# Retention layer of a hybrid decoder: four sample states updated during the attention, queries weighed on VectorE

## The reference, cut to what matters

```python
q = _rotate(...); k = _rotate(...) * (RET_DK ** -0.5)
o = intra + inter                     # prompt: chunks; sample: one token
# for a sample (T = 1) this is, per head, with g = 1 - 2**(-5-h):
#   S_new = g * S_old + k^T v         (256 x 512), stored
#   o     = q @ S_new                 (512)
o = o * rsqrt(mean(o * o) + EPS)
o = o.reshape(B, T, vd) * silu(gate)
return o @ w_out, S
```

## Time and profile before

| | |
|---|---|
| Time, median of 3 runs | 2841.74 us (2841.07 to 2852.38) |
| The profiled execution's own time | 2859.43 us |
| Its span | 2857.9 us |
| TensorE busy (matmul) | 2704.7 us, 95% |
| VectorE busy | 1282.3 us, 45% |
| ScalarE busy | 796.0 us, 28% |
| GpSimd busy | 288.5 us, 10% |
| Mean granted TensorE clock | 0.963 |
| Chain that ended last | PE 87%, DVE 7%, issue 3%, ACT 2% |

### The profile page before, as it was taken

How to read it: one execution, slowest core, us unless ns; L and a number is a source line. 1 busy time by engine, 2 the same in 40 slices (tenths; PEclk the granted TensorE clock), 3 DMA queues, 4 the chain that set the end, 5 groups by cost and what they waited for, 6 DMA issues and landing times.

```text
span 2857.9 us, 49322 instructions
## 1 busy us (share of the span) xinstructions
PE 2704.7 (95%) x20961; PEld 2591.1 (91%) x20961; DVE 1282.3 (45%) x1577; ACT 796.0 (28%) x935; POOL 288.5 (10%) x305
## 2 busy tenths in 40 slices
PE   7999999999999999999999999898879888999997
PEld 6999997989898899999999999788878787999997
DVE  5444234535353554433444423665546654544333
ACT  3222222323232432222322222332223222322222
POOL 1000010101010110000100000004410342100000
PEclk9999999999999999999999999998989899999998
DMA  4332333525152433322333223220012100233231
GB/s 120 88 88 84 87 101 109 174 66 182 60 182 66 141 89 88 88 80 86 111 96 95 79 79 107 70 69 21 25 65 75 47 30 19 77 99 89 70 91 61
DMA packets 340962, 246.82 MB, mean 86 GB/s; under 512 B 9540, under 2 KB 322044, under 8 KB 340832
## 3 DMA queue, kind: packets, MB, share of 16 engines
q1 hardware_dynamic: 326480, 197.32, 23.6%
q0 software_dynamic: 14352, 47.58, 5.0%
HBM read 218.81 MB, written 26.05 MB: 86 GB/s over the span
## 4 chain that ended last, share of the span: by engine, by line
PE 87%; DVE 7%; issue 3%; ACT 2%; DMA 0%; SPq 0%; POOLq 0%; POOL 0%; ACTq 0%; DVEq 0%
PE ps L684 57%; PE ps L864 13%; PE ps L1024 6%; PE ps L785 2%; PE ps L756 1%; PE ps L762 1%; DVE cv L1699 1%; ACT wh L1164 1%; PE ps L721 1%; DVE wl L1417 1%; PE ps L975 1%; PE ps L982 0%; PE ps L987 0%; DMA raw<-in_ffn_gu_dram 0%; PE ps L1070 0%
## 5 line engine op out<-in xcount | busy, mean ns | idle before, releaser
L1417 DVE TENSOR_TENSOR wl<-raw,wh 128x2048 fp32r<-128x2048 f32 (+1 forms) x204 | 427.5, 2095 | 389.6 <-ACT wh L1164 389.6
L684 PE MATMUL ps<-xh,wh 128*128 128x260 f32 x2816 | 569.5, 283 | 4.7 <-DVE gate L1882 4.4
L684 PE MATMUL ps<-xh,wl 128*128 128x260 f32 x2816 | 568.6, 284 | 0.0
L684 PE MATMUL ps<-xl,wh 128*128 128x260 f32 x2816 | 567.9, 283 | 0.0
L1164 ACT ACTIVATE wh<-raw 128x2048 fp32r<-128x2048 f32 (+1 forms) x204 | 354.4, 1737 | 355.9 <-PE ps L684 224.9
L684 PEld LDWEIGHTS ps<-xh,wh 128*128 128x128 f32 x2816 | 435.9, 189 | 6.3 <-issue 5.2
L684 PEld LDWEIGHTS ps<-xh,wl 128*128 128x128 f32 x2816 | 435.5, 189 | 0.0
L684 PEld LDWEIGHTS ps<-xl,wh 128*128 128x128 f32 x2816 | 434.3, 189 | 0.0
L684 PE MATMUL ps<-hh,wh 128*128 128x260 f32 x1408 | 287.9, 286 | 13.4 <-DVE hl L1887 13.4
L684 PE MATMUL ps<-hh,wl 128*128 128x260 f32 x1408 | 286.0, 285 | 0.0
L684 PE MATMUL ps<-hl,wh 128*128 128x260 f32 x1408 | 285.9, 285 | 0.0
(11 more groups left out here) (326 smaller groups left out, 3016.5 us busy)
## 6 DMA issues: line engine op xcount, KB each, us to landing
raw<-in_ffn_gu_dram SPq DMA_DIRECT2D x176, 512.0 KB, 5.0
raw<-in_ffn_down_dram SPq DMA_DIRECT2D x64, 384.0 KB, 3.5
raw<-in_ret_w_in_dram SPq DMA_DIRECT2D x48, 512.0 KB, 4.5
raw<-in_ffn_down_dram SPq DMA_DIRECT2D x64, 320.0 KB, 4.0
s_ring<-in_state_ret_dram POOLq DMA_DIRECT2D x32, 512.0 KB, 4.7
out_dram<-s_ring POOLq DMA_DIRECT2D x32, 512.0 KB, 5.1
raw<-in_gdn_w_in_dram SPq DMA_DIRECT2D x32, 512.0 KB, 4.6
raw<-in_ret_w_out_dram SPq DMA_DIRECT2D x16, 512.0 KB, 4.4
```

Source lines behind the costliest of these rows:

```text
L684: m_ = nc.tensor.matmul(ps[:, 2 * q + h, 0:HALF], w_, v[:, kt0 + t, h * HALF:(h + 1) * HALF], start=b_, stop=e_)
L1417: nc.vector.tensor_tensor(wl[:, s, 0:cols], raw[:, s, 0:cols], wh[:, s, 0:cols].bitcast(F32), ALU.subtract).then_inc(w_low, 1)
```

## The change

- Values 0 to 3 are spread after the prompt's outputs 1 and 2, into banks 0 to 3. Values 4 and 5 take the old place of 0 and 1, values 6 and 7 stand in gate unit 9.
- States 0 to 3 are decayed before the v copies of ScalarE, updated by VectorE during the prompt's outputs and sums, and stored by GpSimd's queue between its sums of squares. All four places of the ring are reloaded after the last sum.
- VectorE weighs each updated state with the query: c is half 0 times q's first 128 values, d is half 1 times the other 128 plus c. The sum lies in `sq`, `ssq`, a spare place under `yh`, or `osum`. TensorE then sums over partitions with a column of ones: four tiles of weights, not eight.
- Queries 0 to 3 stand in gate unit 8, queries 4 to 7 in unit 10, each in twos; the samples' norm comes one step of 128 earlier in unit 11.
- u and w are now the two instructions of an update, each counted.

```diff
-RET_T = Steps("p0 p1 p23 k01 v0 v1 v2 k23 v3 vs o0 o1 o2 o3 s0 s1 n "
-              "b0 b1 b2 b3 q0 q1 b4 b5 q2 q3 b6 b7 q4 q5 q6 q7 ns")
-RET_V = Steps("q k pt0 pt1 pt23 k01 k23 vlo ro u0 u1 on0 u2 u3 y0 lo0 on1 u4 u5 y1 lo1 on2 u6 u7 y2 lo2 on3 "
+RET_T = Steps("p0 p1 p23 k01 v0 v1 v2 k23 v3 vs o0 o1 b0 b1 o2 b2 b3 o3 s0 s1 n "
+              "b4 b5 q0 q1 q2 q3 b6 b7 q4 q5 q6 q7 ns")
+RET_V = Steps("q k pt0 pt1 pt23 k01 k23 vlo u0 w0 u1 w1 c0 c1 d0 d1 u2 w2 u3 w3 c2 c3 d2 d3 ro "
+              "on0 u4 w4 u5 w5 c4 c5 d4 d5 y0 lo0 on1 u6 w6 u7 w7 c6 c7 d6 d7 y1 lo1 on2 y2 lo2 on3 "
...
-RET_A = Steps("v0 v1 v2 v3 vs o0 sq0 o1 sq1 o2 sq2 o3 sq3 s0 s1 root "
-              "g0 g1 g2 g3 silu0 hi0 g4 g5 silu1 hi1 g6 g7 silu2 hi2 rs silu3 hi3")
+RET_A = Steps("g0 g1 g2 g3 v0 v1 v2 v3 vs o0 sq0 o1 sq1 o2 sq2 o3 sq3 s0 s1 root "
+              "g4 g5 silu0 hi0 g6 g7 silu1 hi1 silu2 hi2 rs silu3 hi3")
...
+        def weighed(b):
+
+            return (sq[:, 0, 0:RV], sq[:, 1, 0:RV], ssq[:, 0:RV], spare[:] if b < RING else osum[:])[b % RING]
+
+        def value_bank(b):
+
+            return b if b < RING else 4 + b % 2
...
 # GpSimd
+                    if e >= 2:
+                        for b in (2 * e - 4, 2 * e - 3):
+                            store(b)
...
+                for c in range(RING):
+                    pool.wait_ge(s_stored[c], 32 * h + 16)
+                    pool.wait_ge(ret_v, RET_V(f"d{c}", h))
+                    pool.sem_inc(pool_held, 1)
+                    pool.dma_start(s_ring[:, c], state(ret_in, c + RING)).then_inc(s_landed[c], 16)
...
+                for b in range(RING, DEC):
+                    store(b)
...
 # TensorE
+                    if e in (1, 2):
+                        value(2 * e - 2)
+                        value(2 * e - 1)
...
-                    pe.wait_ge(ret_v, RET_V(f"u{b}", h))
+                    pe.wait_ge(ret_v, RET_V(f"d{b}", h))
                     for e in range(4):
-                        for t in range(2):
-                            m_ = nc.tensor.matmul(ps[:, 7, e * DEC + b:e * DEC + b + 1],
-                                                  s_ring[:, b % RING, t, e * P:(e + 1) * P],
-                                                  rq[:, t, SEQ + b:SEQ + b + 1], start=t == 0, stop=t == 1)
+                        m_ = nc.tensor.matmul(ps[:, 7, e * DEC + b:e * DEC + b + 1], weighed(b)[:, e * P:(e + 1) * P],
+                                              ones[:, 0:1], start=True, stop=True)
...
                     if g == 0:
                         in_products(*unit, range(0, 2))
+                        query(0)
+                        query(1)
                         in_products(*unit, range(2, 5))
+                        query(2)
+                        query(3)
...
+                    elif g == 1:
+                        in_products(*unit, range(0, 5))
+                        value(6)
+                        value(7)
...
+                    elif g == 2:
+                        in_products(*unit, range(0, 2))
+                        query(4)
+                        query(5)
+                        in_products(*unit, range(2, 5))
+                        query(6)
+                        query(7)
...
+                        in_products(*unit, range(0, 6))
                         pe.wait_ge(ret_v, RET_V("ossq", h))
...
 # ScalarE
+                act.wait_ge(head_landed, 16 * h + 16)
+                for b in range(RING):
+                    decay(b)
                 for c in range(4):
                     act.wait_ge(ret_t, RET_T(f"v{c}", h))
...
+                    for b in ((4, 5), (6, 7), (), ())[g]:
+                        decay(b)
...
+                    if g == 0:
+                        act.wait_ge(ret_t, RET_T("q3", h))
...
 # VectorE
+                def weigh(b, half):
+
+                    if half == 0:
+                        if b >= RING:
+                            dve.wait_ge(ret_t, T(f"q{b - RING}", h))
+                        dve.wait_ge(ret_v, V(f"u{b}", h))
+                        nc.vector.tensor_scalar(weighed(b), s_ring[:, b % RING, 0, :], rq[:, 0, SEQ + b:SEQ + b + 1], None, ALU.mult)\
+                            .then_inc(ret_v, V.did(f"c{b}"))
+                    else:
+                        dve.wait_ge(ret_v, V(f"c{b}", h))
+                        nc.vector.scalar_tensor_tensor(weighed(b), s_ring[:, b % RING, 1, :], rq[:, 1, SEQ + b:SEQ + b + 1], weighed(b),
+                                                       ALU.mult, ALU.add).then_inc(ret_v, V.did(f"d{b}"))
...
+                update_two(0)
+                update_two(2)
                 split_next(4)
...
-                    if g < 3:
-                        update(2 * g + 2)
-                        update(2 * g + 3)
+                    if g < 2:
+                        update_two(2 * g + 4)
```

More of the change, by code:

```diff
@@ L343, in build @@
             rinv_s = sb("rinv_s", [P, DEC], stack=st)
+            with ExitStack() as before_yh:
+                spare = sb("spare", [P, RV], stack=before_yh)
             yh = sb("yh", [P, 4, NTOK], F32R, stack=st)
@@ L534, in ret_body, with store @@
                     pool.dma_start(s_ring[:, b], state(ret_in, b)).then_inc(s_landed[b], 16)
+                def store(b):
+                    pool.wait_ge(ret_v, RET_V(f"w{b}", h))
+                    pool.sem_inc(pool_held, 1)
+                    pool.dma_start(state(ret_new, b), s_ring[:, b % RING]).then_inc(s_stored[b % RING], 16)
                 for e in range(4):
                     pool.wait_ge(ret_a, RET_A(f"sq{e}", h))
+                    if e >= 2:
+                        for b in (2 * e - 4, 2 * e - 3):
+                            store(b)
                     if e == 0:
@@ L751, in ret_body, with value @@
                 pe.wait_ge(ret_a, RET_A("vs", h))
+                def value(b):
+                    if b == 0:
+                        pe.wait_ge(ret_v, RET_V("vlo", h))
+                    elif b in (4, 5):
+                        pe.wait_ge(ret_a, RET_A(f"s{b - 4}", h))
+                    elif b in (6, 7):
+                        pe.wait_ge(ret_v, RET_V(f"w{b - 2}", h))
+                    both = pick[:, b:b + 1].broadcast_to([LOW + DEC, P])
+                    nc.tensor.matmul(ps[:, value_bank(b), :], both, vst[:], start=True, stop=True)\
+                        .then_inc(ret_t, RET_T.did(f"b{b}"))
                 for e in range(4):
-                    if e == 3:
-                        pe.wait_ge(ret_v, RET_V("vlo", h))
                     for jb in range(4):
@@ L820, in ret_body @@
                         m_.then_inc(ret_t, RET_T.did("ns"))
-                        in_products(*unit, range(7, KT)).then_inc(parts_done, 1)
-                    if g < 3:
-                        value(2 * g + 2)
-                        value(2 * g + 3)
+                        in_products(*unit, range(6, KT)).then_inc(parts_done, 1)
                 slot(6)
@@ L1501, in ret_body, with update, update_two @@
                     .then_inc(ret_v, V.did("vlo"))
+                def update(b):
+                    dve.wait_ge(ret_t, T(f"b{b}", h))
+                    dve.wait_ge(ret_a, A(f"g{b}", h))
+                    for t, name in ((0, "u"), (1, "w")):
+                        st_ = s_ring[:, b % RING, t, :]
+                        nc.vector.scalar_tensor_tensor(st_, ps[:, value_bank(b), :], rk[:, t, SEQ + b:SEQ + b + 1], st_,
+                                                       ALU.mult, ALU.add).then_inc(ret_v, V.did(f"{name}{b}"))
+                def weigh(b, half):
[9 more added lines that the diff above has]
+                                                       ALU.mult, ALU.add).then_inc(ret_v, V.did(f"d{b}"))
+                def update_two(b):
+                    for n in range(2):
+                        update(b + n)
+                    for half in range(2):
+                        for n in range(2):
+                            weigh(b + n, half)
+                update_two(0)
+                update_two(2)
                 split_next(4)
@@ L1504, in ret_body @@
                 nc.vector.reciprocal(rinv_o[:], rinv_o[:]).then_inc(ret_v, V.did("ro"))
-                def update(b):
-                    dve.wait_ge(ret_t, T(f"b{b}", h))
-                    dve.wait_ge(ret_a, A(f"g{b}", h))
[L1509 to L1513, removed]
                 def sample_outputs(e, gated, high):
```

42 lines of the change are left out of this document (11 added, 31 removed).

## The result

The changed kernel takes 2829.14 us (median of 20 runs, 2817.16 to 2842.67), the kernel before 2848.19 us (20 runs, 2840.48 to 2855.57). The ratio is 0.9936, with a 95% interval of 0.9921 to 0.9951: about 19 us or 0.64% faster. The forecast was 32 us faster. The profiled execution took 2833.71 us, 25.7 us less than that of before.

A forecast was written before the change was run, and what follows sets the result against it. TensorE was taken to bound the retention heads. Gains of 53 us less 15.3 of waits and 5 of clock gave 33 us, profiled 2826; less 17.7 for the median, 2810 was predicted, range 2797 to 2831.

The forecast's parts named there:

- (a): TensorE's queries load 4 tiles instead of 8: 0.85 us less each, 27.2 us over 32 queries.
- The blocks of VectorE: Two updates, two multiplies at 0.47 us and two multiply-adds at 0.75 us: 4.76 us for a block of two.
- The walk: Second head step by step: VectorE becomes the bound behind unit 8; TensorE waits 3.8 us a head, 15.3 us in all.
- Reloads: States 4 to 7, asked for by POOL from 640.1: first ready by 646.5, wanted at 654.4, 8 us of cover.
- (c): Slow clock once per head behind the last four queries, 51.2 us at 0.50, no longer falls: 23 us gained.
- its charge: Clock falls at the samples' norm in somewhat over half of the heads, staying low 3.7 to 7 us: 5 us lost.
- the two gaps looked at: TensorE without products 2.65 us around queries 6 and 7, taken as harmless, and 3.5 us at the samples' norm.
- 2.5 us of cover: GpSimd's last sum ends at 640.1, the norm product wants it at 642.66; each us beyond 2.5 costs 4.
- R1: Rival: clock in the heads still falls as long as before; gain 15 us, 2827 us; chance 0.12.
- R4: Rival: VectorE's operations in two blocks stretched by sharing ports with GpSimd; 25 us slower, 2867 us; chance 0.04.

The follow-up runs named there:

- The doubled queries: Changed kernel with each tile of queries 0 to 3, or in another run 4 to 7, multiplied twice: 2850.95 us and 2835.43 us.
- the control with the moved split: Kernel before, with VectorE's split of slot 7 behind the residual additions of output units 12 and 13: 2846.41 us, ratio 1.0003.
- the filled waits: Changed kernel with 11 unused products of 512 columns ahead of TensorE's wait for the samples' norm: 2818.72 us, ratio 0.9896.
- the paired queries: Kernel before with early values and updates of states 0 to 3 and queries in twos, but no weighing: 2877.23 us, ratio 1.0086.
- the sums first: Changed kernel with GpSimd's stores of states 2 and 3 behind its last sum of squares: 2815.78 us, ratio 0.9896.
- the products at the turns: Changed kernel with three times three unused products in the waits between the turns of v and the prompt's outputs: 2815.07 us, ratio 0.9885.

## Why the prediction was right in sign and too high

What held, by its own steps:

- **(a), the queries.** 256 instructions fewer, 8 for a query, 0.81 and 0.89 us from a start to the next (646.08, 646.89, 647.78), 0.85 in the mean.
- **The blocks of VectorE.** c 0.478 us (0.47), d 0.745 (0.75), updates 0.743 (0.74).
- **The walk.** VectorE starts as soon as value 0 is there. Behind unit 8 it is the bound: forecast waits of 0.95 us at query 6 and 2.67 at the norm, measured 1.1 and 2.8 (starts 1.19 and 2.91 apart where 0.12 is the pace). With yl2 about 16 us, not 15.3. The forecast's own sum has a small slip here: 653.8 and 20.6 are 674.4, not 674.2, which leaves 3.2 us of waits, not 3.62. VectorE's chain from unit 8 to the norm was forecast at 23.8 us and took 23.8 to 24.0. The doubled queries show it apart from the profile.
- **Reloads.** ScalarE starts on states 4 and 5 at 645.10, VectorE uses them from 650.83: hidden, as forecast. "SBUF — State Buffer", SBUF: two separate sides, in the Trainium skill warns of DMAs issued by GpSimd while VectorE runs a one-input operation in its two-port mode. The trace agrees in kind: the stores' issue takes 0.605 us on average, not 0.534, and two of them 1.60 us at 633.17, beside c for states 2 and 3. For the reloads it costs nothing; these two issues stand ahead of the late sum.

What failed is the size of three terms. The first is by far the largest.

- **The clock, (c) less its charge: 23 - 5 = 18 us forecast, about 7.5 measured.** The (c) of 23 us came: the long stretch behind the queries is gone. "I take it that ... the second makes the clock fall in somewhat over half of the heads" was about right in number, three of four, but each fall lasted 6.8 us, not 5: 20.4 us at 0.50, 9 us and not 5. What the forecast put at nothing is every fall outside the two gaps looked at. The stretch between the turns and the outputs shows one in four heads before and four in four after (one to three in the kernels of the experiments that have no added products there), and one more stands in a first unit: 13.6 us at 0.50 more, 6 us. That makes 23 - 9 - 6 = 8 us in the profile, and 17 us of slow stretches or 7.5 us over many runs, not the 40 of the forecast. That the profile of before was a slow one (0.963 against a mean of 0.9668, and above all of the 20 runs) is not the reason: the control with the moved split, at 0.967, has 58 us at 0.50 in its heads. The clock does follow what TensorE does; that the filled waits and the paired queries show, with 10 us won and about 22 of 31 lost.
- **The wait of the norm product for GpSimd's sum: "2.5 us of cover" forecast, 0.8 to 1.0 us a head lost, 3.6 us.** From the end of update 3 (633.3) to the end of the sum (638.77) the forecast had 2.0 us, one issue and 1.27; it took 5.4, two issues and 3.98. The price of the sum was taken from a time when VectorE was idle beside it. "GPSIMD Engine Reference", Key points, in the Trainium skill says that GpSimd shares its SBUF interfaces with VectorE, with contention where VectorE's instruction has two SBUF inputs or is in a two-port mode. The trace agrees, with 3.98 us for 1.27.
- **The wait at the third output unit: not in the forecast, 5.1 us of waits at the output products in the profile against 1.9 before, so 3 us.** The forecast reckoned the slow products behind 687.83 as pure gain. They hid a wait of VectorE's order.

With these the sum is 27 + 3 - 16 - 4 - 3 + 7.5 = 14.5 us; 19 were measured. Fewer changes from one kind of product to another (about 0.5 us a head by the starts) give 2 us of the rest; 2 to 3 us stay open.

Of the rivals, none came as told. R1's time, 2827 us, is near, but its mechanism, "the clock still falls as long as before", is wrong: the stretch behind the queries is gone. That 2829 us lies in the stated range, near its upper end, is luck for this reason: the range was drawn to hold most of R1. R4, the same ports, came in another place and small, in the changed kernel on GpSimd's side and not on VectorE's.

## What to carry to other kernels

Where a wait or a slow clock goes, ask what comes early now and what it then waits for, here two additions that stand behind a split in VectorE's order. Price an operation of GpSimd by a row in which VectorE works as it will beside it. And when slow stretches of TensorE's clock are a part of the sum, read the mean granted clock of many runs and not one trace: here 0.01 of it was 25 us, more than the change. Ask of each stretch, too, which engine is the bound where it stands: behind the queries, in VectorE's part, 3.4 us at half clock cost nothing, at the outputs they cost 1.7 us.

## What was not expected of the hardware

- The clock fell with TensorE busy without a break: 32 one-column fp32 products, 3.4 us, twice in a row with dense products between them, gave 126 us at 0.50 in four heads. Behind 16 in a row, 1.7 us, the changed kernel's profile has no fall, but those with the sums first and with the products at the turns have one in each head, behind queries 6 and 7, ahead of which TensorE had waited 0.9 us.
- Eleven useless products of 512 columns, 2.67 us in a wait, made the kernel 10 us faster.
- An fp32 addition of 128x512 on GpSimd took 3.98 us beside two-input operations of VectorE, 1.27 without. In the kernel with the early updates alone it began beside a lone split, and there the split paid, 3.60 us for 2.28:

```profile
642.06 3.60 DVE L1448 TENSOR_TENSOR wl<-raw,wh 128x2048 fp32r<-128x2048 f32 x1 [2.68 <-ACT wh L1188]
```

```profile
642.23 1.28 POOL L565 TENSOR_TENSOR osum<-osum,rot 128x512 f32<-128x512 f32 x1
```

- VectorE's one-input multiply suffered too: 1.17 to 1.41 us for 0.48 in each of the four heads, beside a sum in the kernel with the sums first.
